# The first projection of each layer reads the stream before it is normalized, and weight tiles alternate slots across the layers

## The reference

```python
def hybrid_layer(x, ...):
    h = rmsnorm(x, norm_g)          # x * rsqrt(mean(x*x) + eps) * norm_g, per token
    proj = h @ w_in                 # 1024 x 11168
    (a_b, a_c, a_x, a_z, c_q, c_kv, k_pe, b_z, dq, dk, dv, c_z, gate_pre) = split(proj)
    q  = rmsnorm(c_q, q_a_norm_g) @ w_uq          # c_q: 256 columns
    kv = rmsnorm(c_kv, kv_a_norm_g) @ w_ukv       # c_kv: 128 columns, k_pe: 32 columns
    ...                                           # two attentions, a convolution, gates
    return x + merged @ w_o
```

## Time and profile before

| | us |
|---|---|
| median of 3 runs | 1992.64 (1989.52 to 1994.97) |
| the profiled execution's own time | 1993.92 |
| its span, first to last instruction | 1992.0 |
| layer 0: first quarter of `lora` to the start of layer 1's | 18.5 to 420.9 |
| layer 1 | 420.9 to about 815 |
| block and experts | about 815 to 1992.0 |

### The profile page before, as it was taken

How to read it: one execution, slowest core, us unless ns; L and a number is a source line. 1 busy time by engine, 2 the same in 40 slices (tenths; PEclk the granted TensorE clock), 3 DMA queues, 4 the chain that set the end, 5 groups by cost and what they waited for, 6 DMA issues and landing times.

```text
span 1992.0 us, 26961 instructions
## 1 busy us (share of the span) xinstructions
PE 1888.7 (95%) x10968; PEld 1193.8 (60%) x10968; DVE 749.3 (38%) x1417; ACT 581.2 (29%) x1051; POOL 522.7 (26%) x220
## 2 busy tenths in 40 slices
PE   7999999989999999989899999999999999999997
PEld 6779889977799899744474444343334443333443
DVE  4785563447854644544534212121112121211212
ACT  4554445445544455322412111011011110110111
POOL 5766556767674557200000000000000000000000
PEclk9999999999999999999989999999999999999999
DMA  8555333555553234621548999999999999999995
GB/s 304 191 174 207 128 107 118 205 182 201 181 194 134 97 127 170 221 85 43 206 157 367 429 427 430 428 428 429 428 429 427 428 428 428 429 428 429 428 429 234
DMA packets 111413, 563.43 MB, mean 283 GB/s; under 512 B 4768, under 2 KB 24352, under 8 KB 86464
## 3 DMA queue, kind: packets, MB, share of 16 engines
q1 hardware_dynamic: 111328, 562.21, 70.5%
HBM read 561.15 MB, written 1.05 MB: 282 GB/s over the span
## 4 chain that ended last, share of the span: by engine, by line
PE 61%; DMA 28%; DVE 7%; ACT 2%; issue 1%; SPq 0%; DVEq 0%; ACTq 0%
DMA ring<-in_e_in_dram 28%; PE bank L1708 15%; PE score L927 11%; PE bank L1698 10%; PE bank L749 4%; PE mixed L965 4%; PE bank L1675 3%; PE bank L850 2%; PE mixed L1792 1%; PE flip L1775 1%; DVE ring L2280 1%; PE bank L988 1%; PE score L1761 1%; PE score L948 1%; PE flip L1733 1%
## 5 line engine op out<-in xcount | busy, mean ns | idle before, releaser
L2087 POOL TENSOR_TENSOR w_lo<-ring,w_hi 128x1024 fp32r<-128x1024 f32 (+1 forms) x216 | 522.5, 2431 | 285.2 <-ACT w_hi L1986 284.6
L927 PE MATMUL score<-ring,space 128*64 128x512 f32 x2016 | 452.7, 594 | 38.4 <-DMA ring<-in_e_in_dram 37.2
L927 PEld LDWEIGHTS score<-ring,space 128*64 128x64 f32 x2016 | 141.6, 137 | 338.4 <-issue 248.6
L1986 ACT ACTIVATE w_hi<-ring 128x1024 fp32r<-128x1024 f32 (+1 forms) x216 | 226.8, 1051 | 219.3 <-PE bank L1708 120.5
L1708 PE MATMUL bank<-h_hi,w_hi 128*128 128x256 f32 x896 | 261.9, 292 | 0.0
L1708 PE MATMUL bank<-h_lo,w_hi 128*128 128x256 f32 x896 | 254.2, 284 | 0.0
L1708 PE MATMUL bank<-h_hi,w_lo 128*128 128x256 f32 x896 | 254.0, 283 | 0.0
L965 PE MATMUL mixed<-ring,space 128*64 128x512 f32 x1024 | 226.8, 595 | 0.3 <-ACT space L1183 0.3
L1179 ACT ACTIVATE space<-space 128x512 f32<-128x512 f32 x32 | 20.2, 632 | 695.7 <-DVE space L1482 695.7
L1482 DVE TENSOR_SCALAR space<-score 128x512 f32<-128x512 f32 x32 | 22.2, 693 | 411.1 <-PE score L927 411.1
L1708 PEld LDWEIGHTS bank<-h_hi,w_hi 128*128 128x128 f32 x896 | 172.6, 193 | 4.5 <-issue 4.4
(11 more groups left out here) (341 smaller groups left out, 2351.0 us busy)
## 6 DMA issues: line engine op xcount, KB each, us to landing
ring<-in_e_in_dram SPq DMA_DIRECT2D x126, 2048.0 KB, 25.1
ring<-in_e_out_dram SPq DMA_DIRECT2D x64, 2048.0 KB, 22.1
ring<-in_w_in_dram SPq DMA_DIRECT2D x42, 2048.0 KB, 7.8
ring<-in_w_ada_dram SPq DMA_DIRECT2D x16, 1024.0 KB, 5.3
ring<-in_w_o_dram SPq DMA_DIRECT2D x6, 2048.0 KB, 8.0
ring<-in_w_qkv_dram SPq DMA_DIRECT2D x4, 2048.0 KB, 10.0
ring<-in_w_ada_dram SPq DMA_DIRECT2D x4, 2048.0 KB, 7.9
ring<-in_w_out_a_dram SPq DMA_DIRECT2D x2, 2048.0 KB, 7.9
```

The source lines that it names most:

```text
L927: ins = pe.matmul(score[HALF * blk:HALF * blk + HALF, which * W:(which + 1) * W], xs[:, 2 * j + r, HALF * hh:HALF * hh + HALF], wk[:, blk ...
L1986: act.activation(split_part(w_hi, k), raw_part(k), ACT.Copy).then_inc(hi_done, 1)
L2087: pool.tensor_tensor(split_part(w_lo, k), raw_part(k), split_part(w_hi, k), ALU.subtract).then_inc(lo_done, 1)
```

## The change

`lora` no longer reads the normalized stream. ACT rounds x·norm_g (not divided by the root of the mean square) into `raw_hi` (`raw_high`), DVE forms `raw_lo` (`raw_low`), and `lora`'s products are made of these. Since a token's factor is common to its row of the result, it is multiplied in afterwards: `token_scales` takes each token's factor out of `rsx` with the identity matrix (a product and a reduction) into `token_rs`, ACT's squares of `lora` take it as their scale, and DVE's multiplications of `lora`'s bank take it as a second factor. Half of the raw pieces, and the first two quarters of weights, are made in the last unit of the layer before; the others between the sums. The first `dq` unit now waits quarter by quarter for `hready`. The two turns of `lora` move from behind quarters 6 and 7 to behind quarters 9 and 10. `NT` becomes 27: tile 0 of layer 1 takes the slot of tile 25 and is issued when that has been split; tile 0 of the block likewise.

```diff
-NT = 28
+NT = 27
...
-        TURN[LONG_AT[n_ + (1 if n_ == 0 else 2)], 4 - len(made) + i_] = v_
+        TURN[LONG_AT[n_ + 2], (3 if n_ == 0 else 4) - len(made) + i_] = v_
...
+        raw_hi, raw_lo = latent_r[:, 0:DC, :], latent_r[:, DC:2 * DC, :]
+        token_rs = stat[:, 1, 0:TT]
...
+        def raw_slot(l, tl):
+            return (l * NT + tl) % LRING
...
-                        sp.wait_ge(lo_done, split_count(LAYERS - 1, NQ - 1))
+                        sp.wait_ge(lo_done, split_count(LAYERS - 1, NQ - 1 - 4 * (LRING - 1 - n)))
...
-                if m == NT - 1:
-                    m -= LRING
...
-                sp.dma_start(dst, src).then_inc(landed[n % LRING], 16)
-            def slot(n):
-                return ring[:, n % LRING, :].rearrange("p (c n) -> p c n", c=DC)
+                sp.dma_start(dst, src).then_inc(landed[raw_slot(l, n)], 16)
...
-                slot_free(l, NT - 1)
-                sp.sem_inc(landed[(NT - 1) % LRING], 16)
...
-                if kind in ("lora", "out"):
-                    pe.wait_ge(hready, l * 8 + (0 if kind == "lora" else 4) + q + 1)
+                if kind == "lora":
+                    pe.wait_ge(raw_ready, l * 4 + q + 1)
+                elif kind == "out" or QUARTER[u] == 4:
+                    pe.wait_ge(hready, l * 8 + (4 if kind == "out" else 0) + q + 1)
+                x_hi, x_lo = (raw_hi, raw_lo) if kind == "lora" else (h_hi, h_lo)
...
+                        if kind == "lora":
+                            act.wait_ge(token_ready, l + 1)
+                            squares_of_both(l, u, 384, [token_rs[:, t:t + 1] for t in range(TT)])
+                        else:
+                            squares_of_both(l, u, W)
...
+            def raw_high(l, i):
+                layer_now[0] = l
+                for c in (2 * i, 2 * i + 1):
+                    ins = act.activation(raw_hi[:, c, :], x[:, c, :], ACT.Copy, scale=l_("norm_g", c, 1))
+                ins.then_inc(raw_rounded, 1)
...
             act.wait_ge(par_ready, 1)
+            for i in range(3):
+                raw_high(0, i)
+            split_to(0, 1)
             for l in range(LAYERS):
                 layer_now[0] = l
-                split[0] = 0
                 act.wait_ge(score_free, l * NS + 2)
                 act.activation(rsx, varx, ACT.Sqrt).then_inc(rsx_ready, 1)
+                raw_high(l, 3)
+                split_to(l, PARTS)
                 for n in range(4):
-                    split_to(l, min(n + 1, PARTS))
+                    split_to(l, PARTS + n + 1)
                     stream_high(l, n, normed_x)
                 evacuate(l, 0)
...
                     squares_of_x(l + 1, i)
+                    if l + 1 < LAYERS and i == 1:
+                        raw_high(l + 1, 0)
+                        raw_high(l + 1, 1)
+                        split[0] = 0
+                        split_to(l + 1, 2)
+                if l + 1 < LAYERS:
+                    split_to(l + 1, PARTS)
+                    raw_high(l + 1, 2)
...
+            def raw_low(l, i):
+                now, layer_now[0] = layer_now[0], l
+                dve.wait_ge(raw_rounded, l * 4 + i + 1)
+                for c in (2 * i, 2 * i + 1):
+                    ins = dve.scalar_tensor_tensor(out=raw_lo[:, c, :], in0=x[:, c, :], scalar=l_("norm_g", c, 1),
+                                                   in1=raw_hi[:, c, :], op0=ALU.mult, op1=ALU.subtract)
+                ins.then_inc(raw_ready, 1)
+                layer_now[0] = now
+            def token_scales(l):
+                own = qn[0][:, 0:T].rearrange("p (t n) -> p t n", t=TT)
+                link(dve.tensor_tensor(own, rsx.rearrange("p (t n) -> p t n", t=TT),
+                                       c_("ident").unsqueeze(1).broadcast_to([P, TT, P]), ALU.mult))
+                dve.tensor_reduce(token_rs, own, AX.X, ALU.add).then_inc(token_ready, 1)
...
+                    own = token_rs[:, t:t + 1]
+                    link(dve.tensor_scalar(kpe[:, t, :], b[:, 384:416], own, None, ALU.mult))
+                    link(dve.tensor_scalar(q[:, 0:256], b[:, 0:256], rs[:, r:r + 1], own, ALU.mult, ALU.mult))
+                    dve.tensor_scalar(q[:, 256:384], b[:, 256:384], rs[:, r + 1:r + 2], own, ALU.mult,
...
+            for i in range(2):
+                raw_low(0, i)
             for l in range(LAYERS):
                 base[0] = l * PER["layer"] + start
                 steps[0] = 0
                 layer_now[0] = l
                 dve.wait_ge(scored, l * NS + 1)
                 dve.tensor_scalar(varx, score[:, 0:T], 1.0 / D, EPS, ALU.mult, ALU.add).then_inc(score_free, 1)
+                raw_low(l, 2)
                 dve.wait_ge(rsx_ready, l + 1)
                 link(dve.reciprocal(rsx, rsx))
+                raw_low(l, 3)
                 for n in range(4):
                     for c in (2 * n, 2 * n + 1):
                         ins = dve.scalar_tensor_tensor(out=normed_x[:, c, :], in0=x[:, c, :], scalar=l_("norm_g", c, 1),
...
                     ins.then_inc(stream_ready, 1)
                     if n:
                         stream_low(l, n - 1, normed_x)
+                    if n == 1:
+                        if l == 0:
+                            dve.wait_ge(loaded, 16)
+                        token_scales(l)
                 stream_low(l, 3, normed_x)
...
                 for u in range(FILL, NU):
+                    if l + 1 < LAYERS and u == NU - 2:
+                        raw_low(l + 1, 0)
+                        raw_low(l + 1, 1)
                     evacuate(l, u)
```

More of the change, by code:

```diff
@@ L100 @@
 PER_BANK = (NU - len(SHORT)) // BANKS
-assert (NU - len(SHORT)) % BANKS == 0 and len(SHORT) % 2 == 0 and NT % LRING == 0
+assert (NU - len(SHORT)) % BANKS == 0 and len(SHORT) % 2 == 0 and LAYERS * NT % LRING == 0
 NORMED = [u for u, x in enumerate(UNITS) if x[0] in ("lora", "dq", "mq", "mkv", "dk")]
@@ L215 @@
 CP, NCP = places(CONSTS)
-CHAINED = dict(layer=111, pair=2, job=2)
+CHAINED = dict(layer=112, pair=2, job=2)
 def slope(g, h):
@@ L1611, in _ @@
                     width = W if n else LORA
-                    tile(l, n, slot(n)[:, :, 0:width], columns(wl, a, width))
+                    tile(l, n, slot(l, n)[:, :, 0:width], columns(wl, a, width))
                     if n == 0 and l == 0:
@@ L1618, in _ @@
                 for b, wb in enumerate((w_out_a, w_out_b, w_out_c)):
[L1619 removed]
+                    tile(l, 22 + b, ring[:, raw_slot(l, 22 + b), :].rearrange("p (c n) -> p c n", c=4),
                          wb[bass.ds(l, 1)].rearrange("a (c p) n -> p (a c) n", p=P))
@@ L1622, in _ @@
                 for n in range(2):
-                    tile(l, 25 + n, slot(25 + n), columns(wol, n * W, W))
+                    tile(l, 25 + n, slot(l, 25 + n), columns(wol, n * W, W))
                 if l + 1 < LAYERS:
@@ L1696, in quarter @@
                             c = 2 * q + i
-                            for x_, w_ in ((h_hi, w_hi), (h_hi, w_lo), (h_lo, w_hi)):
+                            for x_, w_ in ((x_hi, w_hi), (x_hi, w_lo), (x_lo, w_hi)):
                                 ins = pe.matmul(b[:, 0:n], x_[:, c, t], w_[:, k % PARTS, i, 0:n],
-                                                start=c == 0 and x_ is h_hi and w_ is w_hi,
-                                                stop=c == DC - 1 and x_ is h_lo)
+                                                start=c == 0 and x_ is x_hi and w_ is w_hi,
+                                                stop=c == DC - 1 and x_ is x_lo)
                     else:
@@ L1866, in squares_of, with squares_of_both @@
                 act.activation(square[:, 0:width], src, ACT.Square).then_inc(squares, 1)
-            def squares_of_both(l, u, width):
+            def squares_of_both(l, u, width, scales=(1.0, 1.0)):
                 act.wait_ge(squares_used, l * NG + MEAN_OF[u] + 1)
                 act.wait_ge(unit_done, done(l, u))
-                act.activation(square2[:, 0, 0:width], bank_of(u)[:, 0:width], ACT.Square)
+                act.activation(square2[:, 0, 0:width], bank_of(u)[:, 0:width], ACT.Square, scale=scales[0])
                 act.wait_ge(unit_done, done(l, u + 1))
-                act.activation(square2[:, 1, 0:width], bank_of(u + 1)[:, 0:width], ACT.Square).then_inc(squares, 1)
+                act.activation(square2[:, 1, 0:width], bank_of(u + 1)[:, 0:width], ACT.Square,
+                               scale=scales[1]).then_inc(squares, 1)
             def root(l, u):
@@ L1918, in evacuate @@
                     if who[-1] == 0:
-                        squares_of_both(l, u, 384 if kind == "lora" else W)
+                        if kind == "lora":
[3 more added lines that the diff above has]
+                            squares_of_both(l, u, W)
                         root(l, u)
```

23 lines of the change are left out of this document (11 added, 12 removed).

## The result

| | before | changed |
|---|---|---|
| median, first series (12 runs of before, 11 of the change) | 1990.85 us | 1996.2 us |
| ratio, with its 95% interval | | 1.0023 (1.0015 to 1.0032) |
| the same kernel again (26 runs of before, 12 of the change) | 1990.58 us | 1995.53 us |
| ratio, again | | 1.0020 (1.0009 to 1.0030) |
| span of the profiled execution | 1992.0 us | 1993.8 us |

The change makes the kernel 4 to 5 us slower, within the 6 us of the forecast's "no change". One further run of the change in the first series, 2715 us long at a mean granted clock of 0.65, is left out; why it was slow isn't known.

The account below looks back on a forecast made before the run. PE, busy for 95% of 1992.0 us, was taken to bound the kernel. Layer 1 at -1.6, layer 0 at +0.8 and the clock at +3.4 sum to +2.6 us, on the median of 1992.64 that is 1995.2; range 1987 to 2000.

Parts of the forecast that it names:

- no change: Whole kernel: the forecast itself, a change within 6 us of either sign, given 72%.
- What it takes away: Start of `lora`: it runs at once behind `ada`, 7.5 us earlier in layer 1, 3.3 us in layer 0.
- What it adds: DVE's chain to the last `h_lo`: added instructions wait for POOL, ending 6.3 us later in layer 1, at 434.1.
- Quarters 4 to 7: First `dq` unit, layer 1: PE waits for late `h_lo` or ACT; quarter 7, rounded behind `lora`'s root, starts at 439.3.
- the two terms -1.9 and +0.5: Start of quarter 7, before counting the turn: layer 1 keeps 1.9 us of its gain, layer 0 loses 0.5 us.
- The turns: First turn of `lora`, 0.33 us, no longer ahead of quarter 7: leaves -1.6 us in layer 1, +0.8 in layer 0.
- The clock: Behind PE's 2.9 us wait ahead of quarter 7: a fall to half level in both layers, +3.4 us, bounds 0 and 3.4.
- The tile at nothing: Earlier tile of layer 1 and of the block: costs nothing, as ACT waits for no landing in the boundary.
- The rival of a late tile: Quarter 0 not rounded before the sum: `lora` about 1 us later, quarter 7 not, about 1995 us; 6%.
- The gain stays: Rival: waits for POOL don't pile up, quarter 7 comes without a wait, sum -10.8 us, about 1982; 12%.
- Two more turns: Rival: DVE loses two more turns to POOL per layer, quarter 7 later than 443, 12 us slower, about 2005; 10%.

Follow-up runs that it names:

- the tiles alone: The kernel before with only the change's new round of 27 tiles, `lora` still reading the normalized stream: 1989.96 us, ratio 0.9995 to before.
- the reciprocal and the sums in PSUM: Changed kernel with the root's reciprocal in PSUM: 1989.81 us, 0.9997; with sums of squares there too and quarters 7 and 8 rounded ahead of the root: 1985.42 us, 0.9967.
- the token scales last: Changed kernel with the two small instructions making the per-token scales moved behind the last h_lo: 1998.87 us, ratio 1.0033 to before.

## Why the forecast was right, point by point

The forecast was 1995.2 us in a range of 1987 to 2000, with 78% for a change within 0.3%; it came to 1995.5 and 1996.2 us, with +2.6 us forecast and +4.0 and +4.6 measured (by the ratios; +5.0 and +5.3 by the medians). That the forecast in us was hit within 1 us is partly luck: its base, the median of three runs, lay about 2 us above the medians of 12 and 26 runs. So is the size of the sum, in which a clock term that was too large stands against a cost that is missing. The mechanism, a gain at `lora` that is lost again at quarter 7, was right. Times of layer 1 below are less 4.06 us, the lateness at the first of its sums (416.42 against 412.36).

- **What it takes away.** `lora` of layer 1 from 415.9 to 425.2 forecast: 415.85 to 425.1. In layer 0 the end at 27.0: 26.9. Right.
- **What it adds.** The four h_lo at 423.7, 429.9, 431.3 and 434.1: they ended at 423.75, 429.8, 431.2 and 434.0. Wrong inside it: the second pair of raw instructions was not held up (0.88 us for the two), so that normalization began at 419.75, not 421.5; its first four instructions then took 3.40 us beside the same GpSimd instruction and ended at the same point.
- **Quarters 4 to 7** at 426.5, 429.9, 433.6 and 439.3, root at 435.7: 426.7, 430.0, 433.5, 439.2 and 435.5. In layer 0, last h_lo, root and quarter 7 at 34.2, 35.7 and 39.4: 34.2, 35.7 and 39.36. Right, and with it the two terms -1.9 and +0.5.
- **The turns** were put at +0.3 us in each layer, and this is the term that was mis-sized. At their new place they cost that, and they no longer fill the wait ahead of quarter 7. The turns at their old place gave 6 us (3 to 9), perhaps most of it clock.
- **The clock** was put at +3.4 us, a fall in both layers for certain. The mechanism was right and the number too firm: of the five waits of 2.6 us in the profiles of this study two were followed by a fall, that is 1.4 us for both layers, not 3.4. That the sum still came out 1.4 to 2 us low, not high, says that something else costs 3 to 4 us which the forecast doesn't have. PE's waits in the layers account for 0 to 2 us of it (24.6 and 26.5 us in the two profiled executions of the change, 24.5 in that of before), and the average time at the lower clock for next to nothing (24.3 to 24.5 us in the runs of before, 24.1 and 25.0 in the change's). Where the rest goes isn't settled.
- **The tile at nothing**: shown by the tiles alone, 0.9995. The rival of a late tile fell as well, for ScalarE waits for no landing from 405 to 445 us.
- **The rivals.** "The gain stays" fell: quarter 7 has a wait. "Two more turns" fell too, with quarter 7 at 439.2 and not behind 443. That the vector engine's waits for GpSimd are what eats the gain was argued in the forecast from a few rows; the reciprocal and the sums in PSUM showed it. What the forecast named as a rule of the code (quarter 7 only behind the root) and didn't price by itself is ScalarE's order; changing it alone brings the change to 0.9991 (0.9981 to 1.0000), a gain at the edge of the noise.

## What to carry to other kernels

Where a change starts one engine earlier, walk the others' queues with the waits that the earlier start brings, and look for an instruction that stands behind a wait which it doesn't need: here a rounding behind a root cost about 6 us. Then look for what the moved instruction itself waits for: quarter 8 ahead of the root made the root wait for a landing. Beside a busy GpSimd put one of two operands of a vector instruction into PSUM, even the operand of a tiny one. And don't clear a wait of its filler: here two waits of 0.89 and 1.18 us were better than one of 2.60 us by some 6 us, probably because the long one takes the clock with it more often.

## What the runs showed of the hardware that was not expected

**A tiny instruction with a single tensor operand waits too.** Two means of 128x2 from SBUF to SBUF took 3.54 and 3.55 us beside GpSimd, 0.36 us with their input in PSUM. The forecast had the rule for two operands only, and had taken the 1.67 us of the earlier trace rows as one more case of it. It isn't every instruction with one operand: with quarter 7 ahead of the root the two reductions (128x2, from SBUF) just ahead of these means took 0.68 and 0.42 us beside the same GpSimd instructions, as without them. The Trainium skill ("SBUF — State Buffer", section "Who interferes with whom") says that a tensor_scalar can enter a mode that uses both of the vector engine's port pairs, on conditions for its operands, and then can contend with GpSimd. The rows of the means agree with it.

**One for one.** As long as GpSimd's instructions follow each other without a rest, the vector engine gets in one excluded instruction per instruction of GpSimd, about 2.4 us each (two in 4.78 us; an h_lo pair in 4.91 us). A faster supply of GpSimd can therefore slow the vector engine, as the token scales last showed.

**How often a wait takes the clock.** Over all fourteen profiled executions, by the granted clock in the 4 us behind a wait of PE in the layers:

| PE's wait before | falls | of |
|---|---|---|
| 2.0 to 3.5 us (for `ada`'s weights, at 15 us) | 10 | 14 |
| 4.1 to 4.9 us (for `h_lo` or a quarter) | 6 | 6 |
| 2.6 us (quarter 7) | 2 | 5 |
| 2.2 us (attention) | 10 | 28 |
| 1.75 us (attention) | 9 | 28 |
| 1.6 to 1.7 us (quarters 4 and 8) | 0 | 10 |
| 1.4 us (attention) | 0 | 28 |
| 1.1 us (one turn before the attention) | 0 | 28 |
| 1.9 to 3.1 us, elsewhere at layer 0's start | 0 | 5 |
| 0.8 to 1.4 us, at a layer's start | 5 | 12 |

Three of the five in the last row are in the first 20 us of the kernel, where the clock had fallen behind `ada`'s wait already, and the other two are one fall behind neighbouring waits (the turns at their old place). For the same reason the wait of 1.57 us at 18.52 in the kernel before isn't in the table. The falls aren't independent of one another: of the ten behind 2.2 us nine came in a layer where the wait of 1.75 us, 27 us earlier, had taken the clock too. Nor does a fall need a wait of PE: during or within 4 us behind 32 matmuls of 128x2 (3.63 us, at 190.35 in the kernel before) it came in 26 of 28 cases. A fall costs 1.7 us where PE has work. The 56 attention waits of 1.75 and 2.2 us are in every version alike, and by themselves make two executions of one program differ by several us.
